# Contraction-split 8 KB weight pieces, a ring of three and four gather buffers in a hybrid attention and expert kernel

## The reference

```python
sb_q, sb_k, sb_v, nsa_q, ..., merge_g = split(x @ w_in)
o_sb, o_nsa, o_moba = three attentions of 4 heads of 32
g = sigmoid(merge_g).reshape(B, S, 3, 1024)
mix = g[:,:,0]*(o_sb @ w_br_sb) + g[:,:,1]*(o_nsa @ w_br_nsa) + g[:,:,2]*(o_moba @ w_br_moba)
x = layer_norm(ALPHA * x + mix @ w_out)
q = x @ w_q; s1, s2 = q against two tables of 128 keys, per head
idx, g = the 8 best pairs of each of 4 heads      # 32 experts of 16384 per token
act = gelu(dot(u_tab[idx], x))
x = layer_norm(ALPHA * x + sum((g * act) * v_tab[idx]))
```

## Time and profile before

| | us |
|---|---|
| three runs | 3117.9, 3130.63, 3136.47 (median 3130.63) |
| the profiled execution, own time | 3131.75 |
| its span in the trace | 3130.0 |
| TensorE clock granted, mean | 0.869 of 2.4 GHz |

### The profile page before, as it was taken

The page is one execution under the profiler, slowest core; times in us unless marked ns, Lnnn a source line. Parts: engine busy times, 40 slices in busy tenths (PEclk is TensorE's granted clock), DMA queues, the critical chain, the costliest instruction groups (busy, mean ns, idle before and its releaser), DMA issues.

```text
span 3130.0 us, 30645 instructions
## 1 busy us (share of the span) xinstructions
PE 2377.8 (76%) x10920; PEld 1576.5 (50%) x10920; DVE 2023.9 (65%) x4057; ACT 764.9 (24%) x1507; POOL 1281.5 (41%) x1028
## 2 busy tenths in 40 slices
PE   8998868958998887798697886985899899773000
PEld 4664656744544465576454564673454456462000
DVE  0122274786886458558874685487886468759888
ACT  2342212203434222221233210311444232110000
POOL 0000063553651036435661356164554024725776
PEclk9998989977988899899899998996999999886555
DMA  4222288886874369888894589696787348977998
GB/s 143 86 83 81 88 325 310 295 292 200 307 276 157 95 207 331 321 275 320 307 338 157 204 319 376 228 346 212 244 281 251 121 165 310 388 242 259 329 356 307
DMA packets 383544, 776.99 MB, mean 248 GB/s; under 512 B 20768, under 2 KB 242080, under 8 KB 383008
## 3 DMA queue, kind: packets, MB, share of 16 engines
q0 software_dynamic: 147456, 536.94, 47.5%
q1 hardware_dynamic: 233056, 227.79, 22.4%
q10 hardware_dynamic: 2880, 10.31, 0.8%
HBM read 766.56 MB, written 8.39 MB: 248 GB/s over the span
## 4 chain that ended last, share of the span: by engine, by line
PE 50%; DMA 17%; DVE 14%; POOL 10%; issue 6%; ACT 2%; SPq 1%; DVEq 0%
PE ps L914 15%; DMA wring<-in_merge 10%; POOL rows L717 10%; PE ps L768 8%; PE ps L945 6%; DVE x L1366 4%; DMA rows<-in_table_v,idx 3%; PE ps L796 3%; PE ps L755 3%; PE ps L980 3%; PE ps L843 2%; DVE rows L1353 2%; PE ps L1024 2%; PE ps L1006 2%; DMA rows<-in_table_u,idx 1%
## 5 line engine op out<-in xcount | busy, mean ns | idle before, releaser
L717 POOL DMA_INDIRECT rows<-in_table_u,idx x512 | 664.0, 1297 | 949.1 <-DVE idx L1467 465.1
L717 POOL DMA_INDIRECT rows<-in_table_v,idx x512 | 617.3, 1206 | 884.2 <-DVE x L1366 588.7
L914 PE MATMUL ps<-xT,wring 128*128 128x256 f32 x3072 | 797.5, 412 | 201.4 <-DMA wring<-in_merge 158.2
L914 PEld LDWEIGHTS ps<-xT,wring 128*128 128x128 f32 x3072 | 611.5, 205 | 391.7 <-issue 240.8
L1366 DVE SCALAR_TENSOR_TENSOR x<-rows,wts,x 128x1024 f32<-128x1024 f32 x512 | 657.1, 1283 | 85.6 <-DMA rows<-in_table_v,idx 48.7
L1353 DVE CUSTOM_DVE_ANT_0 rows<-rows,x 128x1024 f32<-128x1024 f32 x512 | 616.2, 1224 | 112.8 <-DMA rows<-in_table_u,idx 104.8
L945 PE MATMUL ps<-KA,QA 33*128 33x512 f32 (+7 forms) x576 | 262.7, 553 | 73.8 <-DVE negm_c L1573 54.9
L1228 ACT ACTIVATE scratch<-scratch,negm 128x640 f32<-128x640 f32 (+7 forms) x192 | 143.3, 747 | 487.6 <-DVE negm L1602 471.2
L768 PE MATMUL ps<-wring,G 128*128 128x256 f32 x768 | 194.2, 407 | 31.0 <-DMA wring<-in_w_out_h 24.2
L1602 DVE CUSTOM_DVE_ANT_0 scratch<-ps,cst 128x128 f32<-128x128 f32 (+3 forms) x192 | 87.0, 456 | 200.6 <-PE ps L945 199.7
L768 PEld LDWEIGHTS ps<-wring,G 128*128 128x128 f32 x768 | 151.0, 201 | 84.5 <-issue 52.8
(11 more groups left out here) (181 smaller groups left out, 2515.0 us busy)
## 6 DMA issues: line engine op xcount, KB each, us to landing
wring<-in_merge SPq DMA_DIRECT2D x96, 1024.0 KB
wring<-in_w_out_h SPq DMA_DIRECT2D x24, 1024.0 KB
wring<-in_w_query SPq DMA_DIRECT2D x16, 1024.0 KB
wring<-in_merge SPq DMA_DIRECT2D x16, 768.0 KB
G<-in_w_query SPq DMA_DIRECT2D x12, 1024.0 KB, 11.7
G<-in_x SPq DMA_DIRECT2D x16, 512.0 KB, 5.8
G<-in_ln SPq DMA_DIRECT2D x8, 1024.0 KB, 8.7
rows<-in_table_u,idx POOLq DMA_INDIRECT x512
```

The costliest lines, as they stand in the source:

```text
L717: pool.indirect_dma_start(rows[:, n % GATHER_SLOTS, :], None, tab_u if table == "u" else tab_v, bass.IndirectOffsetOnAxis(ap=idx[:, GT * ( ...
L914: mm = pe.matmul(gate_bank(p)[:, SW * n:SW * (n + 1)], w[:, c, P * n:P * (n + 1)], xT[:, c, SW * (p // HALF_GATES):SW * (p // HALF_GATES + ...
```

## The change

- `RING` 2 to 3, `GATHER_SLOTS` 6 to 4: one slot of 8 KB per partition more, two gather buffers of 4 KB less.
- An item of gate, out and query weights is now 512 output columns over half of the contraction (4 blocks). In DRAM and in SBUF that is one run of 8 KB per partition. Two gates share two items: gate 2m takes item 2m in parts 0 and 1 and item 2m+1 in parts 2 and 3, gate 2m+1 takes them again. The first of a pair is released at half of the second gate (`gate_half`, `query_half`). Matmuls of gate and query keep their number and size; a tile's out projection takes 8 matmuls of 512 columns in place of 16 of 256.
- `G` is [3, 2, 2048], each section's columns for themselves. So rows of x go in runs of 4 KB and the two rows of the norm in runs of 8 KB, and ACT and DVE read `G` without a stride.
- The second gate of the second section (13) moves ahead of the merge, gate 14 to where 13 was, 15 to where 14 was; after the first section's route 8 gates are left, not 9. The merge waits for `HALF_GATES + 2`.

The diff without its context lines; the hunks left out change only how `G` is addressed (tanh, gate, turn, query and match copies on ACT; max, merge, residual add and norm on DVE; match and head turns on PE), with the same instruction counts and shapes.

```diff
@@ -35,14 +35,14 @@
-GATHER_SLOTS = 6
+GATHER_SLOTS = 4
-RING = 2
+RING = 3
...
@@ -189,11 +189,11 @@
-    first += [("merge", 0, k, 1.5) for k in range(12)] + section_outs(0) + gate_steps(HALF_GATES + 1)
-    second = [("norm", 0, 1, 0.0)] + gate_steps(HALF_GATES + 2)
+    first += gate_steps(HALF_GATES + 1) + [("merge", 0, k, 1.5) for k in range(12)] + section_outs(0) + gate_steps(HALF_GATES + 2)
+    second = [("norm", 0, 1, 0.0)] + gate_steps(HALF_GATES + 3)
-    return first, second + sum([gate_steps(p) for p in range(HALF_GATES + 3, GATES)], [])
+    return first, second + sum([gate_steps(p) for p in range(HALF_GATES + 4, GATES)], [])
...
@@ -270,11 +270,11 @@
-            out += [("v", g), ("a", g, 0)] + [("gate", g, p) for p in range(HALF_GATES + 1)]
+            out += [("v", g), ("a", g, 0)] + [("gate", g, p) for p in range(HALF_GATES + 2)]
-            out += [("gate", g, HALF_GATES + 1), ("gate", g, HALF_GATES + 2)]
+            out += [("gate", g, HALF_GATES + 2), ("gate", g, HALF_GATES + 3)]
-            out += [("gate", g, p) for p in range(HALF_GATES + 3, GATES)]
+            out += [("gate", g, p) for p in range(HALF_GATES + 4, GATES)]
...
@@ -389,7 +389,7 @@
-        G = sb("G", [P, 3, KC, GW])
+        G = sb("G", [P, 3, NS, KC * SW])
...
@@ -468,7 +465,18 @@
-            return G[:, 1 + t // 2, :, P * (t % 2):P * (t % 2 + 1)]
+            return G[:, 1 + t // 2, 0, D * (t % 2):D * (t % 2 + 1)]
+        def turned(b, c, t, n=1):
+            f = G[:, b, t // ST, SW * c:SW * (c + n)].rearrange("p (c n) -> p c n", c=n)
+            return f[:, :, P * (t % ST):P * (t % ST + 1)]
+        def row_of(b, t):
+            return G[:, b, t // ST, D * (t % ST):D * (t % ST + 1)]
...
@@ -531,20 +539,21 @@
-                    wide(flat[:, 0:KC * 236]) if kind == "v" else wide(flat[:, 0:KC * P]) if kind == "k" else wide(flat)
+                    wide(flat[:, 0:KC * 236]) if kind == "v" else wide(flat[:, 0:KC * P]) if kind == "k" else \
+                    wide(flat) if kind == "a" else flat
-            view = {"o0": G[:, 0, :, 0:SW], "o1": wide(later), "q0": G[:, 1, :, 0:SW], "q1": G[:, 2, :, 0:SW],
-                    "q2": G[:, 0, :, 0:SW], "q3": wide(later), "k": wide(early[:, 0:KC * P])}[name]
+            view = {"o0": G[:, 0, 0, :], "o1": later, "q0": G[:, 1, 0, :], "q1": G[:, 2, 0, :],
+                    "q2": G[:, 0, 0, :], "q3": later, "k": wide(early[:, 0:KC * P])}[name]
-            return G[:, 2, :, section_columns(sec)]
+            return G[:, 2, SECTIONS[sec][1], :].rearrange("p (b n) -> p b n", b=2)
...
@@ -560,13 +569,19 @@
-                    sp.wait_ge(gate_done, GATES * n + item[2] + 1)
+                    if item[2] % 2 == 0:
+                        sp.wait_ge(gate_half, (GATES * n + item[2]) // 2 + 1)
+                    else:
+                        sp.wait_ge(gate_done, GATES * n + item[2] + 1)
-                    sp.wait_ge(query_done, 4 * n + item[2] + 1)
+                    if item[2] % 2 == 0:
+                        sp.wait_ge(query_half, 2 * n + item[2] // 2 + 1)
+                    else:
+                        sp.wait_ge(query_done, 4 * n + item[2] + 1)
...
@@ -585,14 +600,14 @@
-                    p = item[2] % HALF_GATES
-                    return columns(w_merge[layer, 3 * (p % 4 // 2) + p // 4], 256 * (p % 2), 256 * (p % 2 + 1))
+                    m = item[2] % HALF_GATES // 2
+                    return w_merge[layer, 3 * (m % 2) + m // 2][:, ITEM * (item[2] % 2):ITEM * (item[2] % 2 + 1)]
-                return columns(w[layer, q // 2], 256 * (q % 2), 256 * (q % 2 + 1))
+                return w[layer, q // 2][:, ITEM * (q % 2):ITEM * (q % 2 + 1)]
...
@@ -603,7 +618,7 @@
-                return (x_in if T < TILES else x_mid)[(T % TILES) * P:(T % TILES + 1) * P, :].rearrange("p (c n) -> p c n", c=KC)
+                return (x_in if T < TILES else x_mid)[(T % TILES) * P:(T % TILES + 1) * P, :]
...
@@ -617,14 +632,13 @@
-                    sp.dma_start(x1_T[:, :, P * t:P * (t + 1)], x_src(GT * g + t)).then_inc(resid_landed[t], 16)
+                    sp.dma_start(row_of(1, t), x_src(GT * g + t)).then_inc(resid_landed[t], 16)
-                sp.dma_start(ln1_gb(sec), ln1[layer].rearrange("b (c n) -> (b c) n", n=SW).partition_broadcast(P))\
-                    .then_inc(ln1_landed, 16)
+                sp.dma_start(ln1_gb(sec), ln1[layer].partition_broadcast(P)).then_inc(ln1_landed, 16)
...
@@ -666,7 +680,7 @@
-                for p in range(HALF_GATES + 1):
+                for p in range(HALF_GATES + 2):
...
@@ -676,12 +690,12 @@
-                load("gate", g, HALF_GATES + 1)
+                load("gate", g, HALF_GATES + 3)
-                for p in range(HALF_GATES + 3, GATES):
+                for p in range(HALF_GATES + 4, GATES):
...
@@ -746,7 +760,7 @@
-                        pe.wait_ge(gate_copied, GATES * g + (HALF_GATES + 1 if s_ == 0 else GATES))
+                        pe.wait_ge(gate_copied, GATES * g + (HALF_GATES + 2 if s_ == 0 else GATES))
...
@@ -758,15 +772,16 @@
                 elif kind == "out":
+                    half_c = KC // 2 * (part // 2)
-                    for c in range(KC // 2 * (part % 2), KC // 2 * (part % 2 + 1)):
-                        mm = pe.matmul(piece(sec, kind, k)[:, SW * (q % 2):SW * (q % 2 + 1)], mix_T[:, c, P * t:P * (t + 1)],
-                                       w[:, c, :], start=(c == 0), stop=(c == KC - 1), skip_group_check=True)
+                    for c in range(2 * part, 2 * part + 2):
+                        mm = pe.matmul(piece(sec, kind, k), turned(0, c, t)[:, 0, :], w[:, 512 * (c - half_c):512 * (c - half_c + 1)],
+                                       start=(c == 0), stop=(c == KC - 1))
                 elif kind == "turn":
...
@@ -790,11 +805,14 @@
-                    w = (arrived if part == 0 else held)("q", sec, k)
-                    n = part // 2
-                    for c in range(KC // 2 * (part % 2), KC // 2 * (part % 2 + 1)):
-                        mm = pe.matmul(piece(sec, kind, k)[:, SW * n:SW * (n + 1)], w[:, c, P * n:P * (n + 1)], x1_T[:, c, toks],
-                                       start=(c == 0), stop=(c == KC - 1), skip_group_check=True)
+                    hf, n = part // 2, part % 2
+                    w = (arrived if n == 0 and k % 2 == 0 else held)("q", sec, 2 * (k // 2) + hf)
+                    for c in range(4):
+                        kc, lo = 4 * hf + c, 512 * c + 256 * (k % 2) + P * n
+                        mm = pe.matmul(piece(sec, kind, k)[:, SW * n:SW * (n + 1)], w[:, lo:lo + P],
+                                       G[:, 1, s_, SW * kc:SW * (kc + 1)], start=(kc == 0 and n == 0), stop=(kc == KC - 1), skip_group_check=True)
+                    if part == 1 and k % 2 == 1:
+                        mm.then_inc(query_half, 1)
...
@@ -902,18 +920,21 @@
-                            elif p == HALF_GATES + 1:
+                            elif p == HALF_GATES + 2:
-                        w = (arrived if part == 0 else held)("gate", g, p)
-                        n = part // 2
-                        for c in range(KC // 2 * (part % 2), KC // 2 * (part % 2 + 1)):
-                            mm = pe.matmul(gate_bank(p)[:, SW * n:SW * (n + 1)], w[:, c, P * n:P * (n + 1)],
-                                           xT[:, c, SW * (p // HALF_GATES):SW * (p // HALF_GATES + 1)],
-                                           start=(c == 0), stop=(c == KC - 1), skip_group_check=True)
+                        hf, n = part // 2, part % 2
+                        w = (arrived if n == 0 and p % 2 == 0 else held)("gate", g, 2 * (p // 2) + hf)
+                        for c in range(4):
+                            kc, lo = 4 * hf + c, 512 * c + 256 * (p % 2) + P * n
+                            mm = pe.matmul(gate_bank(p)[:, SW * n:SW * (n + 1)], w[:, lo:lo + P],
+                                           xT[:, kc, SW * (p // HALF_GATES):SW * (p // HALF_GATES + 1)],
+                                           start=(kc == 0 and n == 0), stop=(kc == KC - 1), skip_group_check=True)
+                        if part == 1 and p % 2 == 1:
+                            mm.then_inc(gate_half, 1)
...
```

More of the change, by code:

```diff
@@ L808, in section @@
                         j = 4 * (a % 2) + c
-                        mm = pe.matmul(piece(sec, kind, a)[:, P * c:P * (c + 1)], qp_T[:, j, P * t:P * (t + 1)],
+                        mm = pe.matmul(piece(sec, kind, a)[:, P * c:P * (c + 1)], turned(2, j, t)[:, 0, :],
                                        w[:, j, :], start=True, stop=True, skip_group_check=True)
@@ L825, in head @@
                     for c in range(4):
-                        mm = turn(bank(a % 4)[:, P * c:P * (c + 1)], head_row(t)[:, 4 * hf + c, :])
+                        mm = turn(bank(a % 4)[:, P * c:P * (c + 1)], head_row(t)[:, P * (4 * hf + c):P * (4 * hf + c + 1)])
                     mm.then_inc(x_turned, 1)
@@ L1110, in section @@
                     for b in (2, 1, 0):
```

(23 more changed lines are left out.)

15 lines of the change are left out of this document (5 added, 10 removed).

## The result

| | us |
|---|---|
| changed kernel, median of 5 runs | 3396.4 (3378.9 to 3402.1) |
| kernel before, 5 runs beside it | 3127.5 (3117.9 to 3136.5) |
| ratio | 1.082, 95% interval 1.079 to 1.085 |
| profiled execution after | 3378.9, span 3377.1, clock 0.843 |

8.2% slower; the forecast was 3110, its range ended at 3215. Lines of the changed kernel are shifted: L717 became L731, L914 L933, L1353 L1372, L1366 L1385, L768 L783.

What follows compares the result with a forecast made beforehand. No engine alone bounds the kernel: PE waits for weights and DVE for gathers, with DMA nearly full between route and merge. 3132 - 79 - 43 - 8 + 105 = 3107, rounded to 3110 us; range 3000 to 3215.

Steps and rivals of the forecast that it cites:

- four gather buffers: Tail, bursts and interleaved steps: fewer buffers slow consecutive expert steps, +105 us; +190 at the slow pace, nothing at the fast.
- The pace: Expert steps following each other: 1.65 us each with four buffers against 1.38 with six, taken as +0.26 a step.
- Tail and bursts: Expert steps after the last route, +35 us, and bursts behind each head, +47 us, lose to the slower pace.
- Interleaved steps: Expert steps at a mean pace of 2.4 us: only clusters lose, PE hides half, +23 us.
- Weights, first sections: Merge to route: larger runs and a third slot remove PE's three weight waits and slow restarts, -79 us.
- Route to merge: From the first section's route to the next merge: faster weights, slower gathers, one gate fewer; -43 us, bounds -165 and 0.
- The gain as a whole: Everything but the buffer cost, mainly first sections and the stretches behind the route: 130 us saved.
- Weight waits under 60 us: Sign of being right: PE's waits for weights, 191 us in the cited rows and their like, fall under 60.
- An item in 4 to 6 us: Sign of being right: a weight item lands within 4 to 6 us in the saturated stretches.
- (b): Tail, bursts and stretches behind the route: four buffers starve DVE, pace 1.85, cost +190, about 3190 us; chance 0.30.
- (a): Gathers keep up with four buffers: landing shortens, pace near 1.46, cost +32, about 3035 us; chance 0.25.
- (c): Weight queue: 8 KB runs get no larger share because hardware cuts them, about 3160 us; chance 0.07.

Runs made afterwards that it cites:

- e7: Kernel before with only the gate order changed: gate 13 ahead of the merge, 14 and 15 one place earlier; 3139 us, ratio 1.000.
- e5: Changed kernel with six gather buffers and three ring slots, second norm's gain and bias left out; 3066 us, ratio 0.977.
- e1: Kernel before with four gather buffers in place of six, nothing else changed; 3427 us, ratio 1.093.
- e2: Changed kernel with six gather buffers and two ring slots; 3145 us, ratio 1.002.
- e8: e2 with each 8 KB run of gate, out and query items cut into eight of 1 KB; 3229 us, ratio 1.029.
- e10: e9 with its weight items in runs of 1 KB; 3118 us, ratio 0.995.
- e9: Changed kernel with six buffers, two slots and unshared weight items of 256 columns, packed as 8 KB runs; 3115 us, ratio 0.994.
- e12: e9 with eight gather buffers, second norm's gain and bias left out; 3054 us, ratio 0.974.
- e15: e9 with three ring slots, second norm's gain and bias left out; 3054 us, ratio 0.974.

## Why the prediction was wrong

Stages from the traces, bounded by DVE's first merge of a section and by its writing of the indices of the section's second route (us). A: behind the head's route (in the first group, PE's first gate) up to the merge of the first section, four in all; B: the four first sections; C: first section's route to the next merge; D: second sections; E: the tail. The start (72 to 75) is left out.

| | A | B | C | D | E | span |
|---|---|---|---|---|---|---|
| before | 881 | 853 | 438 | 618 | 267 | 3130 |
| e7, gate moved | 959 | 812 | 405 | 610 | 272 | 3130 |
| e5, the change with six buffers | 968 | 746 | 386 | 615 | 272 | 3059 |
| e1, four buffers alone | 977 | 889 | 470 | 692 | 333 | 3433 |
| changed kernel | 1025 | 785 | 454 | 692 | 344 | 3377 |

(The spans are those of the profiled runs. The kernels with the moved gate have 172 steps in the tail, the other two 166. C before is 438 and not the prediction's 513: the windows of the prediction begin earlier, at the first index write or up to 20 us ahead of it.)

**The step that failed is "four gather buffers", +105.** Alone it is +290 (e1), in the changed kernel +331 (from e5). Its own upper end was +190. Term by term from before to e1:

- The pace. I took 1.65 us a step between 1.38 and 1.85, because landing "holds queueing, which thins as the pace falls". It hardly did: 5.7 us with four against 6.15 with six over the last 128 gathers, where a pace of 1.65 needs 4 x 1.65 - 1.28 - 0.27 = 5.05. In the tail windows a gather goes out every 1.62 us with six buffers and every 2.0 with four: +0.4 a step, tile ends included. The formula at the measured landing gave 1.85 - 1.38 = 0.47 and was near; my 0.26, cut to 0.21 for tile ends, was not.
- Tail and bursts, expected +35 and +47: E +66, D +74. In the tail that is the pace alone, 166 x 0.4 = 66. For the bursts, which lie mostly in D, the same sum gives 202 x 0.4 = 81; that D is the pace too is not shown by itself.
- Interleaved steps, expected +23: A, B and C together +163. This is the larger error. I reasoned that a stretch whose mean pace is 2.4 us loses to a lower buffer pace only in its clusters, and that PE hides half. But DVE takes its expert steps in a fixed place of its program; each wait there delays what stands behind it, a merge, a mask, ACT's copy of a gate, and PE waits for those (the three lines of e1 above, +154).

**"Weights, first sections", -79:** B from before to e5 -108, in the changed kernel -68, since the buffers take 40 of it. Of the 108 the moved gate, which now runs ahead of the section, makes 42 (e7: 812) and gives them back in A; 66 are the weights', near the 79. But their layout hardly moved it (e2: 805, and 8 KB runs for 1 KB 16 us, e8 to e2); the third slot did (e5: 746).

**"Route to merge", -43:** C -52 to e5, and -33 by the gate order alone (e7). But the order's price elsewhere, 28 by my sum, is +78 in A and +5 in the tail against -42 in B and -8 in D: nothing in all. In the changed kernel C is +16, since DVE comes late to its first merge there and PE waits for it (the two windows of after).

**The gain as a whole:** forecast 130, 71 to 75 at six buffers (3137 or 3141 to 3066). What I missed is that two gates sharing their items costs 111 us, which the 8 KB runs (84) and the third slot (79) have to earn back. One path, each step a measured pair: 3137, -19 (e10: order, unstrided rows), +111 (sharing), -84 (8 KB), -79 (slot), +331 (buffers) = 3397. Such a chain of differences has to end at the 3396 of the last kernel; it tells the sizes in this order and proves nothing by closing.

**Signs named in advance.** Weight waits under 60 us: 1.1 for the gates. An item in 4 to 6 us: 6.3 over the whole run. The tail +25 to 45: +78. DVE's waits for gathered rows in the tail, 22 before, over 50: 96 (38.7 and 57.7). POOL's idle from "issue" to DVE: yes. The stretches behind the route end with DVE as the last: yes, by the waits for its merge. "Wrong if DVE waits for rows over 350 us": 575.

**Rivals.** (b) had place and mechanism, four buffers starve DVE, and was too small itself: 3190, with a cost of 190 for 290 to 331 and a gain of 130 for 75. (a), a landing that shortens, fell (its terms add up to 3034, near the 3035 given for it, and not to the 3037 given beside the landing of 3.2 us). (c), that 8 KB runs get no larger share, fell: with the same bytes and order PE waits 242.0 us for gate weights in 1 KB and 90.9 in 8 KB runs (e8, e2). Nor were the runs cut: of the changed kernel's 204340 packets 182304 are under 8 KB, so 22036 are not, against 536 before. The weight of evidence was in the earlier trace rows: six buffers over 7.4 us gave 1.24 under a pace of 1.38, a reserve of a tenth. A resource with so little reserve can't lose a third.

**A version that beats both** with the reference's output is e9: 3115, 8.3% under the changed kernel and 0.6% under the kernel before (0.3 to 1.0%; e10, with runs of 1 KB, is level with it). e12 and e15 say that 8 KB more per partition, spent on either a third slot or two more buffers, would be worth some 50 us more; the second norm's rows, which they leave out, take just that room, and no complete kernel with it was run.

## What to carry over

Before taking buffers from a stream of transfers, work out (landing + use + reissue) / buffers at the landing that the trace shows under load, and don't discount it: here four buffers in place of six shortened it from 6.15 to 5.7 us, not to the 5.05 that my pace needed. Waits of an engine whose order is fixed are paid by everything behind them, so a mean pace with slack in it doesn't protect the interleaved steps. And ask of a layout that makes transfers faster who must now share a buffer for it, and which wait is next: here 132 us of waits for weights went without moving the time.

## What was not expected of the hardware

- One buffer of six is worth 85 us, the next 205; from six to eight at most 13 us with 1 KB runs of weights and 52 with 8 KB.
- With the same bytes on the queue, runs of 8 KB in place of 1 KB took PE's waits for gate weights from 149.3 to 17.1 us (e10, e9), beside a second queue of 4 KB rows, and DVE's waits for these rows from 178 to 224 us. That the gathers lose the share that the weights gain fits both numbers; e15 says that it isn't all of it.
- A gather's landing with four buffers is 5.7 us, 3.75 with half the bytes: by the estimate above 1.8 us fixed and 3.9 us of bytes, three times the 1.3 us worked out for one alone.
